# Split products for eight slots of the first input projection, with GpSimd making the lower weight parts

## The chip, the cores and the metric

The kernel runs on one core of one Trainium2 chip. The metric is the device time of one execution in microseconds. The kernel before takes 1461.06 us, the median of three runs (1459.4 to 1461.32).

## The reference, cut to what matters

Two transformer blocks over 256 tokens of width 1024, all in float32. The change touches the head of the first block:

```
mod = silu(c) @ w_ada + b_ada                  # 6 x 1024 values: shift1, scale1, gate1, shift2, scale2, gate2
h = rms_norm(x, g) * (1 + scale1) + shift1
proj = h @ w_in                                # 1024 -> 2320
q_g, k_g, v_g, a_lr, r_g, q_s, k_s, v_s = split(proj)
o_gla = gated linear attention(q_g, k_g, v_g, log_a(a_lr)); o_gla = rms_norm(o_gla) * silu(r_g)
o_swa = rms_norm(sliding window attention(q_s, k_s, v_s, sinks))
x = x + gate1 * (concatenate(o_gla, o_swa) @ w_out)
x = x + gate2 * peer(modulate(x, shift2, scale2))   # picks 128 experts per token, gathers their rows
```

Everything behind it (the PEER mixer with its gathered experts, a sparse-attention layer, two MLPs and a second attention layer) is untouched.

## The kernel before, in words

Each engine has its program written out by hand, and semaphores order the engines among each other. Weights come in slots of 512 KB (128 partitions x 1024 float32), which SyncE loads into a ring of four buffers. A slot n may be loaded when TensorE has used slot n-4 (`slots_used`).

The first input projection `w_in` has 18 slots, numbered 0 to 17. Each gives one 128 x 256 block of the projection in one half of the PSUM tile `pu` (`entry(e)`, two entries that take turns). ScalarE takes the block out (`evac`), and TensorE may begin slot i only when the blocks up to i-2 are out. `project` and `project_tokens` (lines 672 and 682) multiply in plain float32: eight matmuls of 128x256 (the profile records two for each). `up_slot` (line 709) is the other way, used further on for `w_out`, the MLPs and the second attention layer: the weights and the activations are each split in a high part of the type fp32r and a remainder (`ring_hi`, `ring_lo`, `Xh`, `Xl`), and `three` (line 703) makes three fp32r matmuls for each of the eight. `split_high` (line 450) is two ScalarE copies of 128x512 into `ring_hi`, which has two buffers, so the high part of slot n waits until slot n-2 is used. `split_low` (line 458) is two 128x512 subtractions, in place in the ring; in the kernel before VectorE makes them all.

Beside the slots of `w_in` run the sixteen units of the sliding window attention. From slot 6 (`EARLY`) on, each slot is followed on TensorE and on ScalarE by its share of the attention's steps (`steps_after`: 20 steps over 11 slots, two at most behind a slot). A unit goes from TensorE (scores, L877) to VectorE (bias L2139, maximum L2033), ScalarE (exponential, L1508), VectorE (reciprocal L2038, scaling L2044), TensorE (transposes L887), ScalarE (copy), TensorE (products L899), ScalarE (copy). On ScalarE, the exponentials of the gated linear attention (five activations) stand between the `evac` of slot 5 and that of slot 6.

The modulation is made on VectorE: `modulation` (line 2059) multiplies a row of `w_ada` (512 KB) with `silu(c)` and sums it up. Rows 0 to 15 have buffers of their own, and rows 16 to 39 go through `aring`, four buffers; row n may be loaded when row n-4 is used (`ada_used`). GpSimd issues them all (L542). VectorE takes rows 22 to 33 in the first twelve steps of the attention (`swa_filler`), rows 34 to 37 after the last step, masks the scores of the linear attention (L2157), and takes rows 38 and 39. Behind these in VectorE's order come the lower parts of the first `w_out` slot (L463), the reciprocal of the attention's norm (L2163), the scaling (L2165), the states of the linear attention (L2171, L2174), and then TensorE's products with the states (L1006) and the slots of `w_out`.

After `w_out` come the choice of the experts and 256 gathers of 1 MB each, which GpSimd issues (L581) into ten buffers.

Of the kernel before, what the change touches and what calls it, by code (L numbers as in the profile page):

```python
# [14 lines left out]
P = 128  # L15
# [54 lines left out]
SPLIT, _n = {}, 0  # L70
# [5 lines left out]
XSPLIT = {"w_out": 0, "a_o": 1, "b_in": 3, "b_o": 5}  # L76
# [13 lines left out]
EARLY, BESIDE = 6, 11  # L90

# [28 lines left out]
SEMS = """c_loaded x_loaded cols_loaded relb_loaded small_loaded xn_ready h_scaled h_chunks h2_sq h2_scaled h2_ready tile_done tile_out h2_copied consts_made casts_made c_silu ada_used chain_dve chain_act chain_pool slots_used evacs narrow_psum  # L120
# [10 lines left out]
def build(nc, xT_d, c_d, cols_d, ada_d, weights_d, small_d, alpha_d, keys_d, late_q_d, experts_d, relb_d, onehot_d, sinks_d, fin_row_d, w1_d, out_d):  # L131
    ctx = ExitStack()
    with ctx:
# [211 lines left out]

        def pair_landed(m):

            k = m % PAIR_SLOTS
            before = 0 if k < PAIR_SLOTS - ARING else 16 * ((MOD_EARLY - 2 * C) // ARING)
            return pair_full[k], before + 16 * (m // PAIR_SLOTS + 1)  # L350
# [93 lines left out]
        def tick(g, per_round, base):  # L444

            return base if g is None else g * per_round + base

        halves = (slice(0, 512), slice(512, D))
# [9 lines left out]
        def split_low(eng, api, name, k, g=None):  # L458

            n = SLOT[name] + k  # L460
            for j, half in enumerate(halves):
                eng.wait_ge(s["split_hi"], tick(g, 2 * BODY, 2 * (SPLIT[name] + k) + j + 1))
                api.tensor_tensor(ring_lo[:, n % RING, half], ring[:, n % RING, half],  # L463
                                  ring_hi[:, n % 2, half], ALU.subtract).then_inc(s["split_lo"], 1)
# [7 lines left out]
        def _(sp):  # L472
            for dst, src, sem in ((cols[:, :], cols_d, "cols_loaded"), (relb[0:NB, :], relb_d, "relb_loaded"),
                                  (oneh[0:NB, :], onehot_d, "relb_loaded"), (walr, small_d[:, :, 0:16], "small_loaded"),
                                  (walpha[0:16, :], alpha_d, "small_loaded"), (keysT, keys_d, "small_loaded"),
                                  (sinks[:, :], sinks_d.partition_broadcast(P), "small_loaded")):
                sp.dma_start(dst, src).then_inc(s[sem], 16)
# [31 lines left out]
        def _(pool):  # L509
# [28 lines left out]
            with pool.Fori(2 * C // ARING, MOD_EARLY // ARING) as g:  # L538
                for k in range(ARING):

                    pool.wait_ge(s["ada_used"], g * ARING + (k + 1 - ARING))
                    pool.dma_start(aring[:, k, :], ada_d[bass.ds(g * ARING + k, 1), :, :].rearrange("a p n -> (a p) n"))\  # L542
                        .then_inc(ada_full[k], 16)
# [121 lines left out]
        def _(pe):  # L665
# [33 lines left out]
            def split_ready(name, k, half, g):  # L699

                pe.wait_ge(s["split_lo"], tick(g, 2 * BODY, 2 * (SPLIT[name] + k) + half + 1))
# [151 lines left out]
            pe.wait_ge(s["relb_loaded"], 16 * 2)  # L853
# [118 lines left out]
            project(SLOT["w_in"] + 17, USE["w_in"] + 17, HTf)  # L972
# [526 lines left out]
        def _(act):  # L1499
# [86 lines left out]
            act.dma_start(cs, c_d.partition_broadcast(P)).then_inc(s["c_loaded"], 16)  # L1586
            act.dma_start(XT[:, :, :], xT_d).then_inc(s["x_loaded"], 16)
            act.wait_ge(s["casts_made"], 1)
            act.wait_ge(s["c_loaded"], 16)
            f(cs, cs, ACT.Silu).then_inc(s["c_silu"], 1)  # L1590
            act.wait_ge(s["x_loaded"], 16)
# [66 lines left out]
            evac(SLOT["w_in"] + 17, rs[:, 3, :], entry(USE["w_in"] + 17))  # L1658
            act.wait_ge(s["sums"], NORM["swa"])
# [329 lines left out]
        def _(dve):  # L1989
# [80 lines left out]
            dve.wait_ge(s["cols_loaded"], 16)  # L2070
            first = cols[:, COL["b_ada"]:COL["b_ada"] + 2 * C]
            step(v.tensor_scalar(strided(first[:, 0:1], [[2, C]]), strided(first[:, 0:1], [[2, C]]), 1.0, None, ALU.add))
            dve.wait_ge(s["relb_loaded"], 16 * 2)
# [44 lines left out]
            v.tensor_scalar(kp, kp, 80.0 * GATE_TEMP, None, ALU.min).then_inc(s["ex_ready"], 1)  # L2118

# [40 lines left out]
            modulation(2 * C + 22, 2)  # L2160
            split_low(dve, v, "w_out", 0)
# [680 lines left out]
```

## Time and profile before

| What | Value |
|---|---|
| Median of three runs | 1461.06 us (1459.4 to 1461.32) |
| The profiled execution's own time | 1459.02 us |
| Its span | 1457.4 us |
| TensorE busy | 1295.8 us (89%) |
| VectorE busy | 936.4 us (64%) |
| ScalarE busy | 658.5 us (45%) |
| GpSimd busy | 396.4 us (27%) |
| Granted TensorE clock, mean | 0.983 |

The profile is of one execution. Busy times are sums over the whole span, and engines work beside each other; 1.6 us of the execution's time lie outside the span. The chain of waits follows the work that ended last back from the last instruction, step by step.

### The profile page before, as it was taken

The page shows a single profiled execution, that of the slowest core. Times are in us where ns is not written, and L with a number is a line of the kernel's source. Part 1 is how long each engine was busy: PE and PEld are TensorE (multiplying, and loading weights), DVE is VectorE, ACT ScalarE, POOL GpSimd, SP SyncE. Part 2 cuts the span into 40 slices and gives each one's busy share as a digit, 9 for nine tenths or more (in the row PEclk, how much of TensorE's full clock was granted, in tenths as well). Part 3 has the DMA queues.
Part 4 walks back from the last instruction along what each step waited for, and adds up shares of the span by engine and source line. Part 5 has one row for each costly group of instructions (what it writes and reads, how often), then busy time and mean ns, then how long its engine had stood idle before and what let it go on. Part 6 is the DMA issues. An engine that isn't in the chain of part 4 may idle for free.

```text
span 1457.4 us, 21059 instructions
## 1 busy us (share of the span) xinstructions
PE 1295.8 (89%) x6856; PEld 930.2 (64%) x6856; DVE 936.4 (64%) x2259; ACT 658.5 (45%) x1809; POOL 396.4 (27%) x440
## 2 busy tenths in 40 slices
PE   6999888988888888777787888999999999999998
PEld 3888744434433343222332467899998887899897
DVE  6678787766767666766664566655556744655555
ACT  3444344443443434333433336555545448545554
POOL 4112345544444444444443142200001004100000
PEclk9999999999999999999999998999999999999999
DMA  8877799999999999999999621765556530455554
GB/s 330 339 265 282 272 420 420 421 423 420 421 422 421 420 421 421 422 421 422 421 421 422 246 74 43 255 203 181 184 187 240 193 116 2 159 161 186 186 187 145
DMA packets 81340, 422.50 MB, mean 290 GB/s; under 512 B 10144, under 2 KB 11472, under 8 KB 48368
## 3 DMA queue, kind: packets, MB, share of 16 engines
q0 software_dynamic: 47808, 307.91, 51.6%
q1 hardware_dynamic: 32128, 110.48, 22.7%
q10 hardware_dynamic: 1328, 3.15, 0.6%
q8 instruction: 41, 0.67, 0.2%
q14 instruction: 35, 0.29, 0.1%
HBM read 418.88 MB, written 2.62 MB: 289 GB/s over the span
## 4 chain that ended last, share of the span: by engine, by line
PE 54%; DMA 26%; DVE 11%; ACT 4%; issue 2%; POOL 1%; DVEq 0%; ACTq 0%; SPq 0%; POOLq 0%
DMA big<-in_experts,R 25%; PE pacc L1174 9%; PE pu L705 6%; PE pu L707 6%; PE pu L706 6%; PE pu L678 3%; DVE big L2477 3%; PE pacc L705 2%; PE pacc L706 2%; PE pacc L707 2%; PE pacc L763 2%; PE pacc L762 2%; PE pacc L764 2%; PE pu L688 1%; PE pu L1093 1%
## 5 line engine op out<-in xcount | busy, mean ns | idle before, releaser
L1174 PE MATMUL pacc<-big,early_l 128*128 128x512 f32 x1024 | 481.1, 612 | 106.8 <-ACT early_l L1508 106.8
L1174 PEld LDWEIGHTS pacc<-big,early_l 128*128 128x128 f32 x1024 | 187.3, 193 | 382.7 <-issue 380.2
L2477 DVE CUSTOM_DVE_ANT_0 big<-big,early_h 128x1024 f32<-128x1024 f32 x256 | 310.7, 1225 | 185.9 <-DMA big<-in_experts,R 184.7
L581 POOL DMA_INDIRECT big<-in_experts,R x256 | 289.5, 1131 | 363.6 <-PE pacc L1174 329.4
L463 DVE TENSOR_TENSOR ring_lo<-ring,ring_hi 128x512 fp32r<-128x512 f32 x336 | 220.0, 696 | 193.8 <-ACT ring_hi L456 193.6
L456 ACT ACTIVATE ring_hi<-ring 128x512 fp32r<-128x512 f32 x336 | 192.4, 620 | 135.2 <-PE pu L707 53.1
L1508 ACT ACTIVATE R<-R 128x1 f32<-128x1 f32 x256 | 51.4, 201 | 296.5 <-DVE R L2477 296.3
L705 PE MATMUL pu<-X2h,ring_hi 128*128 128x256 f32 x512 | 146.3, 286 | 3.2 <-DVE big L2592 3.2
L707 PE MATMUL pu<-X2h,ring_lo 128*128 128x256 f32 x512 | 145.5, 284 | 0.0
L706 PE MATMUL pu<-X2l,ring_hi 128*128 128x256 f32 x512 | 145.4, 284 | 0.0
L705 PEld LDWEIGHTS pu<-X2h,ring_hi 128*128 128x128 f32 x512 | 98.8, 193 | 4.3 <-DVE big L2592 3.6
L706 PEld LDWEIGHTS pu<-X2l,ring_hi 128*128 128x128 f32 x512 | 98.9, 193 | 0.3
L1508 ACT ACTIVATE early_l<-early_l,R 128x128 f32<-128x128 f32 x256 | 98.9, 386 | 0.1
L707 PEld LDWEIGHTS pu<-X2h,ring_lo 128*128 128x128 f32 x512 | 98.8, 193 | 0.0
L1508 ACT ACTIVATE early_l<-ident,tk 128x128 f32<-128x128 f32 x256 | 98.7, 387 | 0.0
L705 PE MATMUL pu<-Xh,ring_hi 128*128 128x256 f32 x288 | 85.7, 298 | 7.6 <-DVE Xl L2002 3.2
L707 PE MATMUL pu<-Xh,ring_lo 128*128 128x256 f32 x288 | 82.0, 285 | 0.0
L706 PE MATMUL pu<-Xl,ring_hi 128*128 128x256 f32 x288 | 82.0, 285 | 0.0
L705 PE MATMUL pacc<-act_h,ring_hi 128*128 128x256 f32 x256 | 72.2, 282 | 0.4 <-DVE ring_lo L463 0.4
L706 PE MATMUL pacc<-act_l,ring_hi 128*128 128x256 f32 x256 | 72.0, 281 | 0.0
L707 PE MATMUL pacc<-act_h,ring_lo 128*128 128x256 f32 x256 | 72.0, 281 | 0.0
L1508 ACT ACTIVATE big<-big 128x256 f32<-128x256 f32 (+3 forms) x74 | 34.1, 466 | 78.5 <-DVE big L2592 78.0
(433 smaller groups left out, 2101.1 us busy)
## 6 DMA issues: line engine op xcount, KB each, us to landing
ring<-in_weights SPq DMA_DIRECT2D x208, 512.0 KB, 3.5
big<-in_ada POOLq DMA_DIRECT2D x40, 512.0 KB, 6.4
big<-in_w POOLq DMA_DIRECT2D x12, 512.0 KB, 7.4
big<-in_experts,R POOLq DMA_INDIRECT x256, 19.3
big<-in_late_q POOLq DMA_DIRECT2D x6, 512.0 KB, 8.9
bias_row<-big ACTq DMA_DIRECT2D x1, 1536.0 KB, 19.9
XT<-in_xT ACTq DMA_DIRECT2D x1, 1024.0 KB, 8.2
scr<-in_ada POOLq DMA_DIRECT2D x2, 512.0 KB, 12.2
```

The source lines that it names most:

```text
L456: nc.scalar.activation(ring_hi[:, n % 2, half], ring[:, n % RING, half], ACT.Copy).then_inc(s["split_hi"], 1)
L463: api.tensor_tensor(ring_lo[:, n % RING, half], ring[:, n % RING, half], ring_hi[:, n % 2, half], ALU.subtract).then_inc(s["split_lo"], 1)
L581: pool.indirect_dma_start(out=pair_rows[:, m % PAIR_SLOTS, :], out_offset=None, in_=experts_d, in_offset=bass.IndirectOffsetOnAxis(ap=expe ...
L678: last = mm(entry(e), slot(n)[:, c * P:(c + 1) * P], rhs[:, c, :], start=(c == 0), stop=(c == C - 1))
L705: mm(out, ring_hi[:, n % 2, w], xh, start=start, stop=False, skip_group_check=True)
L706: mm(out, ring_hi[:, n % 2, w], xl, start=False, stop=False, skip_group_check=True)
L707: return mm(out, ring_lo[:, n % RING, w], xh, start=False, stop=stop, skip_group_check=True)
L762: mm(out, xh[:, rows], ring_hi[:, n % 2, w], start=False, stop=False, skip_group_check=True)
L763: mm(out, xl[:, rows], ring_hi[:, n % 2, w], start=False, stop=False, skip_group_check=True)
L1174: last = mm(paccf[:, tt * D + half * 512:tt * D + (half + 1) * 512], diagonal[:, m % 16, :], pair_rows[:, m % PAIR_SLOTS, D + half * 512:D ...
L1508: return nc.scalar.activation(out, in_, func, **k)
L2477: v.tensor_tensor_reduce(out=pair_rows[:, m % PAIR_SLOTS, 0:D], in0=pair_rows[:, m % PAIR_SLOTS, 0:D], in1=h2_rows[:, u % TT, :], scale=1. ...
```

## The change

Slots 6 to 9 and 14 to 17 of `w_in` go through `up_slot` in place of `project`. ScalarE makes their high parts two slots ahead (before the `evac` of slots 4 to 7 and 12 to 15), and the high parts `Xh` of the activations after the `evac` of slots 2 and 3. VectorE makes the lower parts `Xl` before the attention's first step. GpSimd makes the lower parts of the eight slots of weights. GpSimd now issues modulation rows 16 to 25 only, and ScalarE issues rows 26 to 37, each behind a step of the attention, and rows 38 and 39 behind the `evac` of slot 17. `split_no` numbers the split slots for the semaphores, and four semaphores of the first loads are used again for ScalarE's rows. VectorE waits for all sixteen lower parts before it makes the first ones of `w_out`.

```
-SPLIT, _n = {}, 0
+W_SPLIT = (6, 7, 8, 9, 14, 15, 16, 17)
+SPLIT, _n = {}, len(W_SPLIT)
+ACT_ROWS = 26
...
+        def act_row_landed(n):
+            k = n % ARING
+            before = 32 if k == 3 else 16
+            earlier = (n - ACT_ROWS) // ARING
+            return s[("c_then_row0", "x_then_row1", "cols_then_row2", "relb_then_row3")[k]], before + 16 * (earlier + 1)
...
+        def split_no(name, k):
+            return W_SPLIT.index(k) if name == "w_in" else SPLIT[name] + k
...   # GpSimd
-            with pool.Fori(2 * C // ARING, MOD_EARLY // ARING) as g:
-                for k in range(ARING):
-                    pool.wait_ge(s["ada_used"], g * ARING + (k + 1 - ARING))
-                    pool.dma_start(aring[:, k, :], ...).then_inc(ada_full[k], 16)
+            for n_row in range(2 * C, ACT_ROWS):
+                pool.wait_ge(s["ada_used"], n_row + 1 - ARING)
+                pool.dma_start(mod_row(n_row), ada_d[n_row, :, :]).then_inc(ada_full[n_row % ARING], 16)
+            for k in W_SPLIT:
+                split_low(pool, nc.gpsimd, "w_in", k)
...   # TensorE
+                elif i in W_SPLIT:
+                    up_slot("w_in", i, USE["w_in"] + i, None, 0, "w_in" if i == W_SPLIT[0] else None)
...
-            project(SLOT["w_in"] + 17, USE["w_in"] + 17, HTf)
+            up_slot("w_in", 17, USE["w_in"] + 17, None, 0)
...   # ScalarE
+            def row_in(n_row):
+                act.wait_ge(s["ada_used"], n_row + 1 - ARING)
+                sem, landed = act_row_landed(n_row)
+                act.dma_start(mod_row(n_row), ada_d[n_row, :, :]).then_inc(sem, 16)
+            def rows_in(i):
+                if ACT_ROWS <= ACT_ROWS - 1 + i < MOD_EARLY - 2:
+                    row_in(ACT_ROWS - 1 + i)
-            swa_step = attend("swa", swa_out, later=True)
+            swa_step = attend("swa", swa_out, rows_in, later=True)
...
+                if i + 2 in W_SPLIT:
+                    split_high(act, "w_in", i + 2)
...
+                if i in (2, 3):
+                    act.wait_ge(s["h_chunks"], C)
+                    x_high(HTf[:, 4 * (i - 2):4 * (i - 2) + 4, :], i - 2)
...
             evac(SLOT["w_in"] + 17, rs[:, 3, :], entry(USE["w_in"] + 17))
+            row_in(MOD_EARLY - 2)
+            row_in(MOD_EARLY - 1)
...   # VectorE
+                    elif n >= ACT_ROWS:
+                        dve.wait_ge(*act_row_landed(n))
...
             v.tensor_scalar(kp, kp, 80.0 * GATE_TEMP, None, ALU.min).then_inc(s["ex_ready"], 1)
+            both_low("w_in", HTf)
...
             modulation(2 * C + 22, 2)
+            dve.wait_ge(s["split_lo"], 2 * len(W_SPLIT))
             split_low(dve, v, "w_out", 0)
```

## Rows read from the trace of the kernel before

**Rows 1.** The page: GB/s moved in 40 slices of the span.

```profile
GB/s 330 339 265 282 272 420 420 421 423 420 421 422 421 420 421 421 422 421 422 421 421 422 246 74 43 255 203 181 184 187 240 193 116 2 159 161 186 186 187 145
```

**Rows 2.** The chain of waits, 36 to 135 us: start us, us, what.

```profile
43.14 14.01 PE pu L678 x64
...
68.68 3.65 PE pu L678 x16
...
119.05 1.74 PE pacc L969 x8
...
121.33 1.76 DVE R L2163
...
126.46 1.83 PE pacc L1006 x24
```

**Rows 3.** The chain of waits, 135 to 260 us: two split slots of w_out.

```profile
137.80 0.12 PE pu L705
...
143.43 0.12 PE pu L707
```

**Rows 4.** The timeline of ScalarE: start us, us, engine, line, operation, idle before.

```profile
44.05 0.40 ACTq L1612 DMA_DIRECT2D bias_row<-big  x1
...
62.46 3.57 ACT L1508 ACTIVATE big<-big 128x512 f32<-128x512 f32 x5
65.94 0.36 ACT L1508 ACTIVATE big<-pu 128x256 f32<-128x256 f32 x1
...
66.20 0.39 ACT L1508 ACTIVATE big<-big,stats 128x129 f32<-128x129 f32 x1
...
119.09 0.38 ACT L1508 ACTIVATE big<-pu 128x256 f32<-128x256 f32 x1 [0.99 <-PE pu L678]
...
121.75 1.14 ACT L456 ACTIVATE ring_hi<-ring 128x512 fp32r<-128x512 f32 x2
```

**Rows 5.** The timeline of VectorE in and behind the projection.

```profile
64.73 0.15 DVE L2138 COPY big<-sinks 128x1 f32<-128x1 f32 x1 [6.26 <-PE pn L877]
...
70.83 0.15 DVE L2138 COPY big<-sinks 128x1 f32<-128x1 f32 x1
...
126.32 1.22 DVE L2002 TENSOR_TENSOR Xl<-big,Xh 128x1024 fp32r<-128x1024 f32 x1
```

**Rows 6.** Line 638: GpSimd's subtractions' nearest kin; duration ns min/median/max.

```profile
L638 POOL TENSOR_TENSOR big<-big x16: 455/593/737, 875.2 to 888.0; 128x128 f32<-128x128 f32 x8, 128x256 f32<-128x256 f32 x8
```

**Rows 7.** The timeline of GpSimd and VectorE, 1213 to 1216 us.

```profile
1213.37 1.27 DVE L463 TENSOR_TENSOR ring_lo<-ring,ring_hi 128x512 fp32r<-128x512 f32 x2
1213.56 1.44 POOL L655 TENSOR_SCALAR big<-big,stats 128x256 f32<-128x256 f32 x1 [0.35 <-DVE stats L2038]
...
1215.16 0.56 POOL L655 TENSOR_SCALAR big<-big,stats 128x256 f32<-128x256 f32 x1 [0.17 <-DVE stats L2038]
```

**Rows 8.** The timeline, 110 to 120 us: modulation rows 38 and 39.

```profile
110.76 0.53 POOL L542 DMA_DIRECT2D big<-in_ada  x1 [12.20 <-DVE mod L2067]
...
116.08 1.23 DVE L2067 CUSTOM_DVE_ANT_0 big<-big 128x1024 f32<-128x1024 f32 x1 [1.06 <-DMA big<-in_ada]
...
118.36 1.23 DVE L2067 CUSTOM_DVE_ANT_0 big<-big 128x1024 f32<-128x1024 f32 x1 [1.05 <-DMA big<-in_ada]
...
119.51 1.29 DVE L463 TENSOR_TENSOR ring_lo<-ring,ring_hi 128x512 fp32r<-128x512 f32 x2
```

**Rows 9.** DMA issues, 100 to 120 us: KB each, median us to landing.

```profile
ring<-in_weights SPq DMA_DIRECT2D x4, 512.0 KB, 4.0
big<-in_ada POOLq DMA_DIRECT2D x2, 512.0 KB, 5.9
```

**Rows 10.** The timeline of TensorE at 902 us: a start after idle time.

```profile
902.34 0.35 PE L705 MATMUL pu<-Xh,ring_hi 128*128 128x256 f32 x1 [2.46 <-DVE Xl L2002]
```

**Rows 11.** Windows of 1 us: busy PE, PEld, DVE, ACT, POOL; then granted clock, DMA share, GB/s.

```profile
903.00:904.00 1.00, 1.00 (x7) 1.00 (x6) 1.00 (x3) 0.00 (x0) 0.00 (x0) 0.50 0.02 8
...
906.00:907.00 1.00, 1.00 (x10) 1.00 (x9) 0.02 (x1) 0.00 (x0) 0.00 (x0) 0.95 0.00 0
```

More of the change, by code:

```diff
@@ L74 @@
         _n += 4 if _name == "w_out" else _k
-XSPLIT = {"w_out": 0, "a_o": 1, "b_in": 3, "b_o": 5}
+XSPLIT = {"w_in": 0, "w_out": 2, "a_o": 3, "b_in": 5, "b_o": 7}
 RAW = {n: C * i for i, n in enumerate(["mlp0", "kv", "mlp1"])}
@@ L118 @@
 NSA_OUT = OUTNO[SPAN["nsa"][0]]
[L120 removed]
+SEMS = """c_then_row0 x_then_row1 cols_then_row2 relb_then_row3 small_loaded xn_ready h_scaled h_chunks h2_sq h2_scaled h2_ready tile_done tile_out h2_copied consts_made casts_made c_silu ada_used chain_dve chain_act chain_pool slots_used evacs narrow_psum
 narrow_copied z_psum squares sums roots normed la_parts ex_ready ex_done silu_done gla_ops kl_psum kl_copied gla_scores
@@ L344, in pair_column @@
             return u % TT * P + u // TT * TOPK + m % TOPK
+        def act_row_landed(n):
[3 more added lines that the diff above has]
+            return s[("c_then_row0", "x_then_row1", "cols_then_row2", "relb_then_row3")[k]], before + 16 * (earlier + 1)
         def pair_landed(m):
             k = m % PAIR_SLOTS
-            before = 0 if k < PAIR_SLOTS - ARING else 16 * ((MOD_EARLY - 2 * C) // ARING)
+            before = 0 if k < PAIR_SLOTS - ARING else 16 * len(range(2 * C + (k + ARING - PAIR_SLOTS), ACT_ROWS, ARING))
             return pair_full[k], before + 16 * (m // PAIR_SLOTS + 1)
@@ L461, in split_low @@
             for j, half in enumerate(halves):
-                eng.wait_ge(s["split_hi"], tick(g, 2 * BODY, 2 * (SPLIT[name] + k) + j + 1))
+                eng.wait_ge(s["split_hi"], tick(g, 2 * BODY, 2 * split_no(name, k) + j + 1))
                 api.tensor_tensor(ring_lo[:, n % RING, half], ring[:, n % RING, half],
@@ L472, in _ @@
         def _(sp):
-            for dst, src, sem in ((cols[:, :], cols_d, "cols_loaded"), (relb[0:NB, :], relb_d, "relb_loaded"),
-                                  (oneh[0:NB, :], onehot_d, "relb_loaded"), (walr, small_d[:, :, 0:16], "small_loaded"),
+            for dst, src, sem in ((cols[:, :], cols_d, "cols_then_row2"), (relb[0:NB, :], relb_d, "relb_then_row3"),
+                                  (oneh[0:NB, :], onehot_d, "relb_then_row3"), (walr, small_d[:, :, 0:16], "small_loaded"),
                                   (walpha[0:16, :], alpha_d, "small_loaded"), (keysT, keys_d, "small_loaded"),
@@ L699, in split_ready @@
             def split_ready(name, k, half, g):
-                pe.wait_ge(s["split_lo"], tick(g, 2 * BODY, 2 * (SPLIT[name] + k) + half + 1))
+                pe.wait_ge(s["split_lo"], tick(g, 2 * BODY, 2 * split_no(name, k) + half + 1))
             def three(out, n, w, xh, xl, start, stop):
@@ L852, in _ @@
             last.then_inc(s["spreads"], 1)
-            pe.wait_ge(s["relb_loaded"], 16 * 2)
+            pe.wait_ge(s["relb_then_row3"], 16 * 2)
             pe.wait_ge(s["relb_spread"], 1)
@@ L1584, in attend @@
                     one(st)
-            act.dma_start(cs, c_d.partition_broadcast(P)).then_inc(s["c_loaded"], 16)
-            act.dma_start(XT[:, :, :], xT_d).then_inc(s["x_loaded"], 16)
+            act.dma_start(cs, c_d.partition_broadcast(P)).then_inc(s["c_then_row0"], 16)
+            act.dma_start(XT[:, :, :], xT_d).then_inc(s["x_then_row1"], 16)
             act.wait_ge(s["casts_made"], 1)
-            act.wait_ge(s["c_loaded"], 16)
+            act.wait_ge(s["c_then_row0"], 16)
             f(cs, cs, ACT.Silu).then_inc(s["c_silu"], 1)
-            act.wait_ge(s["x_loaded"], 16)
+            act.wait_ge(s["x_then_row1"], 16)
             squares(XT[:, :, :], sq[:, :, :])
@@ L2068, in modulation @@
                                            op0=ALU.mult, op1=ALU.add, accum_out=mod[:, n:n + 1]).then_inc(s["ada_used"], 1)
-            dve.wait_ge(s["cols_loaded"], 16)
+            dve.wait_ge(s["cols_then_row2"], 16)
             first = cols[:, COL["b_ada"]:COL["b_ada"] + 2 * C]
             step(v.tensor_scalar(strided(first[:, 0:1], [[2, C]]), strided(first[:, 0:1], [[2, C]]), 1.0, None, ALU.add))
-            dve.wait_ge(s["relb_loaded"], 16 * 2)
+            dve.wait_ge(s["relb_then_row3"], 16 * 2)
             v.tensor_copy(relb_all[0:NB, :, :], strided(relb[0:NB, 0:1], [[1, NH], [0, P]])).then_inc(s["relb_spread"], 1)
```

2 lines of the change are left out of this document (removed).

## The prediction

> **What bounds the kernel now.** I read the page's throughput slices first. From the sixth slice (about 182 us) to the 22nd (about 800 us) the DMA engines move 420 to 423 GB/s without a break [rows 1]: these are the gathers of the experts, and their number is fixed. They start when the head of the kernel has chosen the first experts. So what moves the head moves the end by as much, and nothing is caught up behind it. The chain of waits says what the head consists of. From 43 to 119 us it is TensorE, slot after slot of the projection [rows 2]; then it leaves TensorE: sums of squares at 119.05, a root on ScalarE, VectorE's reciprocal at 121.33, VectorE's scaling and states, and TensorE again at 126.46. Two facts decide: how early slot 17 ends, and how early VectorE can start that reciprocal. The timeline of VectorE shows that the second has little room: it takes modulation rows 38 and 39 at 116.08 and 118.36, each after idle time for its DMA, then 1.29 us of lower parts until 120.80 [rows 8]. It is free 0.53 us before it is needed.
>
> **The change part by part.**
>
> *Products.* Four plain slots take 14.01 us, 3.50 each [rows 2]. Two split slots of the same shape take 143.55 - 137.80 = 5.75 us, 2.88 each [rows 3]. Eight slots times 0.62 us is 5.0 us of TensorE time, the most that the change can give.
>
> *Activation parts.* VectorE's part is 2 x 1.22 us by the one row of this shape; it falls into the 6.26 us in which VectorE is idle before the first attention unit [rows 5]. ScalarE's part is of the same size, between evacuations of slots 2 to 4. Cost nothing; without the cover it would be up to 2.4 us.
>
> *High parts.* Each slot adds 1.14 us to ScalarE [rows 4], and they stand ahead of evacuations. Those of slots 7 and 8 come before the evacuations of slots 5 and 6, with the five exponentials (62.46 to 66.03) between them. So the evacuation of slot 6 moves from 65.94 by 2 x 1.14 and a little to about 68.5, and the first unit's exponential from 66.20 to about 68.9 [rows 4]. Slot 8 needs that evacuation and began at 68.68 [rows 2]. It can't begin earlier: the 1.24 us that slots 6 and 7 gain are gone. The late exponential also holds up VectorE, whose unit 3 stood at 70.83 [rows 5]; it moves to about 73.2, and TensorE needs it for the scores behind slot 8, whose end stood at 72.33. I put TensorE 1 to 2.5 us behind its old time when it enters the plain slots 10 to 13. Slots 14 to 16 win 1.86 back in part, since VectorE's units are then as tight as TensorE. Slot 17 stands behind the last attention step and gives its full 0.62. I take slot 17's evacuation to end 0.9 us earlier than its 119.47 [rows 4], at 118.5. The bounds are 5.0 us earlier (nothing given back) and 1.5 us later.
>
> *Lower parts on GpSimd.* The trace has no such 128x512 subtraction on GpSimd. Its nearest row runs from 0.46 us at 128 columns to 0.74 at 256 [rows 6]: an estimate of 0.46 + 3 x 0.28 = 1.3 us each, 2.6 us a slot. The lower bound is VectorE's 0.64 us for the same operation [rows 7], the upper twice my value. By 1.3 us a half is ready some 2 us after ScalarE's start and the other 1.3 later. That is on time for slots with attention steps between them, more than 3 us apart, so alone it costs nothing; at twice the price each of the eight slots would wait up to 2 us.
>
> GpSimd and VectorE get in each other's way: a scaling that takes 0.56 us alone takes 1.44 when VectorE has two subtractions of lower parts running [rows 7]. The Trainium skill says why ("SBUF — State Buffer", section "SBUF: two separate sides"): a VectorE operation with two SBUF inputs and a GpSimd operation that reads SBUF exclude each other for a whole instruction. By that rule, every modulation row and every gate product of the linear attention can stand against a GpSimd half. From the row alone, each split slot then costs VectorE up to 1.3 us and GpSimd up to 1.2 in addition; over the four slots 6 to 9 this is at most 5 us, part of it on the path. I take it as the upper half of the 1 to 2.5 us above; it is the third case below in full.
>
> *Modulation rows 26 to 37.* ScalarE's issue is 0.40 us each [rows 4], twelve of them 4.8 us, spread over steps in which ScalarE is half idle. By its order, ScalarE issues row 25+i behind the exponential of unit i, and this waits for VectorE, which has used row 21+i by then: no new wait. They start a little later than now and have three units to land. At most one stall of 1 us in VectorE, nothing on the sum.
>
> *Modulation rows 38 and 39.* Now GpSimd issues row 38 at 110.76, and the two take 5.9 us in the median to land [rows 8, 9]. After the change ScalarE issues them behind the evacuation of slot 17: 118.5 and 118.9. Ring loads of the same size took 4.0 us in this stretch and modulation rows 5.9 [rows 9]; with a ring load and both rows at once I take 4.9 for row 39. It lands at 123.8. VectorE stands at row 38 and then at row 39, with the lower parts and the reciprocal queued behind: 123.8 + 1.2 (row 39) + 1.3 (lower parts) = 126.3, against 121.33. All that follows on VectorE and the states' products on TensorE wait for that: **+5.0 us**. ScalarE's own delay (two issues of 0.40 ahead of the root) is inside it. Nothing hides it, since TensorE has only its filler matmuls there.
>
> *Clock.* TensorE's work ahead of the states' products doesn't wait for the rows and is earlier than before, while those products move from 126.46 [rows 2] to about 131.5; so TensorE gets 5 us or more of idle time. After 2.46 us of idle time the granted clock was 0.50 (1.2 GHz) at 903 and on its way back in the microsecond from 906 [rows 10, 11]. There some three microseconds ran at half speed, which is 1.5 us of work not done. I add **+1.5 us**.
>
> Sum: -0 (the products' gain is inside the 118.5) + 5.0 + 1.5 = +6.5 us on the profiled execution's 1459.02 us, 1465.5. The median of the runs stands 2.04 above the profiled execution, so the forecast is 1467.5 us; I give 1467.
>
> **The rivals.**
>
> *Late rows, but mild.* Slot 17's evacuation ends at 115.5, the rows land in 4 us and the clock doesn't fall. Row 39 is issued at 115.9 and lands at 119.9, and the reciprocal starts at 122.4: +1.1. With half of that luck it is +3. For it: slots 14 to 17 could keep their 2.5 us. Against it: the late exponentials. Time 1462 to 1464.5.
>
> *The shared access decides.* GpSimd's halves and VectorE's rows hold each other up in each of the eight slots, and TensorE waits for second halves. Slot 17 ends 3 to 5 us late (four slots x 1.2 us, less what the plain slots absorb), and the rows come later by the same: +10 to +12, 1471 to 1473. For it: the 1.44 us [rows 7]. Against it: the spaces between the units.
>
> *The products win (other side).* The place is VectorE at the reciprocal. If row 39 were to land before about 115.5, VectorE would be free before the root, and the earlier end of slot 17 would pass: -3 to -5, 1456 to 1458. This decides from an evacuation of slot 17 at about 111, and even the whole 5.0 us of gain brings only 114.5. What could break my reading is time downstream that absorbs the delay, of which rows 1 show none.
>
> *The change doesn't do what it says.* If GpSimd's halves are always the last to come, split slots run no faster than plain ones. This is then the third case with less price, and I leave its chance there.
>
> **How the numbers follow.** Late rows with the clock's fall 0.58 (own range 1464.5 to 1470), mild late rows 0.25, shared access 0.12, products win 0.05. The range 1462.3 to 1472 leaves out the last case, the best of the mild one and the far end of the third. A measurement of this kernel can tell 0.2%, 2.9 us, from no change. Faster by that is the products' case, 0.05. Within it lies half of the mild case, 0.13. Slower is the rest, 0.82.
>
> **What would show it.** L678's groups of 16 are replaced by L705 to L707 of `Xh` in slots 6 to 9 and 14 to 17, 2.9 us each. VectorE's unit 3 stands near 73. In VectorE's timeline, two modulation rows wait for a DMA between 115 and 124, and the reciprocal L2163 starts near 126. TensorE has idle time before L1006, and the granted clock is 0.50 behind it. The first gather comes about 6.5 us later than now, and all behind it by the same. Wrong would be: L2163 before 122, a clock of 1.00 after L1006, or a delay at L1006 that isn't found at the first gather.

## The result, and the profile after

The changed kernel takes 1480.07 us (median of 6 runs, 1476.44 to 1484.22) against 1461.42 us for the kernel before, measured beside it: a ratio of 1.0127 with a 95% interval of 1.0114 to 1.0141. That is 18.7 us slower, where 6 were forecast. The profiled execution took 1480.23 us with a span of 1478.5 us, 21.1 us more than before; its mean granted clock is 0.976 (before 0.983).

The page after, the line that answers to [rows 1] and those on the modulation rows. The gathers run as fast as before and end later. The rows that ScalarE issues have a line of their own now:

```profile
GB/s 330 320 256 214 172 399 416 421 422 421 422 421 421 421 421 421 421 421 421 422 421 422 279 113 47 196 234 183 184 184 208 237 116 12 157 152 188 184 185 144
...
big<-in_ada POOLq DMA_DIRECT2D x26, 512.0 KB, 8.3
...
big<-in_ada ACTq DMA_DIRECT2D x14, 512.0 KB, 4.7
```

The timeline of ScalarE after, beside [rows 4]. The evacuation of slot 6 and the first unit's exponential are 2.15 us later (68.09, 68.35), and the evacuation of slot 17 ends at 126.12. Behind it stand the issues of modulation rows 38 and 39:

```profile
68.09 0.37 ACT L1523 ACTIVATE big<-pu 128x256 f32<-128x256 f32 x1
68.35 0.39 ACT L1523 ACTIVATE big<-big,stats 128x129 f32<-128x129 f32 x1
...
125.74 0.38 ACT L1523 ACTIVATE big<-pu 128x256 f32<-128x256 f32 x1 [0.40 <-PE pu L720]
125.75 0.82 ACTq L1639 DMA_DIRECT2D big<-in_ada  x2
```

The timeline of VectorE after, beside [rows 8]. Two modulation rows (L2102) take 2.29 and 2.28 us where the same row takes 1.22; then come 5.70 us of waiting for row 38, 0.83 for row 39, the lower parts, and the reciprocal:

```profile
117.86 2.29 DVE L2102 CUSTOM_DVE_ANT_0 big<-big 128x1024 f32<-128x1024 f32 x1
120.08 2.28 DVE L2102 CUSTOM_DVE_ANT_0 big<-big 128x1024 f32<-128x1024 f32 x1
...
129.87 1.23 DVE L2102 CUSTOM_DVE_ANT_0 big<-big 128x1024 f32<-128x1024 f32 x1 [5.70 <-DMA big<-in_ada]
131.94 1.23 DVE L2102 CUSTOM_DVE_ANT_0 big<-big 128x1024 f32<-128x1024 f32 x1 [0.83 <-DMA big<-in_ada]
133.09 1.29 DVE L477 TENSOR_TENSOR ring_lo<-ring,ring_hi 128x512 fp32r<-128x512 f32 x2
134.29 1.75 DVE L2200 RECIPROCAL R<-R 128x256 f32<-128x256 f32 x1
```

The chain of waits after, beside [rows 2]: from the evacuation it goes through the DMA of the modulation rows to VectorE's reciprocal, and to the states' products, which took 1.83 us before and take 3.31 now:

```profile
125.74 0.34 ACT big L1523
126.12 5.79 DMA big<-in_ada
...
134.38 1.67 DVE R L2200
...
139.42 3.31 PE pacc L1021 x24
```

TensorE in windows of 2 us, after (busy PE, PEld, DVE, ACT, POOL; granted clock, DMA share, GB/s). In the kernel before the clock is 1.00 from 56 to 136 us. Here TensorE is idle for most of 72 to 76 and of 106 to 108, and its clock falls to 0.50 (1.2 GHz) behind both. VectorE is busy for 1.93 us or more of every two from 72 to 82 us and from 102 to 108 us:

```profile
72.00:74.00 2.00, 0.55 (x5) 0.34 (x3) 1.93 (x8) 0.68 (x3) 1.81 (x1) 1.00 0.72 281
74.00:76.00 2.00, 0.55 (x5) 0.47 (x6) 1.93 (x8) 0.09 (x1) 0.00 (x0) 1.00 0.92 356
76.00:78.00 2.00, 2.00 (x14) 2.00 (x15) 1.93 (x8) 1.05 (x5) 0.00 (x0) 0.71 0.66 209
78.00:80.00 2.00, 2.00 (x11) 2.00 (x11) 1.93 (x8) 0.27 (x2) 0.00 (x0) 0.50 0.83 295
80.00:82.00 2.00, 2.00 (x17) 1.40 (x16) 1.94 (x6) 0.46 (x2) 0.00 (x0) 0.93 0.63 188
...
106.00:108.00 2.00, 0.35 (x2) 0.39 (x4) 1.97 (x5) 0.00 (x0) 0.56 (x1) 0.89 0.87 272
108.00:110.00 2.00, 2.00 (x10) 1.02 (x10) 1.79 (x6) 0.00 (x0) 0.00 (x0) 0.50 0.58 234
110.00:112.00 2.00, 2.00 (x17) 1.67 (x18) 0.00 (x0) 0.94 (x5) 0.00 (x0) 0.75 0.00 0
```

What TensorE waited for, in its own timeline after, are scores (L890). It can't write them before VectorE has read the scores that stand in the same PSUM bank (L2175):

```profile
75.45 0.34 PE L890 MATMUL pm<-big 64*128 64x128 f32 x1 [2.90 <-DVE big L2175]
...
107.65 0.76 PE L890 MATMUL pm<-big 64*128 64x256 f32 x1 [2.31 <-DVE big L2175]
```

How far TensorE had come when it began slot 10, the first of the plain slots in the middle. The lines are of before, of after, and of e13, the changed kernel without the lower parts (see the experiments):

```profile
77.67 3.84 PE L688 MATMUL pu<-ring,big 128*128 128x128 f32 x32
```

```profile
81.76 3.84 PE L701 MATMUL pu<-ring,big 128*128 128x128 f32 x32
```

```profile
78.78 3.84 PE L699 MATMUL pu<-ring,big 128*128 128x128 f32 x32
```

The kernel in five marks, for every kernel of this study (us from the start, from each profiled execution). "w_out" is the first 128x128 product behind the first split slots of `w_out` (before: L1020, behind [rows 3]):

| Kernel | slot 17 out | reciprocal | w_out | first gather | span | ratio of times |
|---|---|---|---|---|---|---|
| before | 119.5 | 121.3 | 143.4 | 164.3 | 1457.4 | 1 |
| after | 126.1 | 134.3 | 160.4 | 183.9 | 1478.5 | 1.0127 |
| e1 rows only | 119.5 | 127.7 | 153.5 | 174.4 | 1471.2 | 1.0083 |
| e2 VectorE makes lower parts | 126.0 | 134.1 | 159.9 | 182.9 | 1476.3 | 1.0119 |
| e3 rows 38, 39 earlier | 125.1 | 130.5 | 156.2 | 177.1 | 1470.6 | 1.0104 |
| e4 50 fillers | 127.8 | 136.0 | 161.1 | 184.5 | 1477.9 | 1.0121 |
| e5 split only | 125.3 | 128.1 | 151.7 | 174.2 | 1468.4 | 1.0065 |
| e6 split 14 to 17 | 121.9 | 125.2 | 150.3 | 172.9 | 1466.4 | 1.0052 |
| e7 split 6 to 9 | 123.2 | 125.1 | 147.2 | 169.7 | 1462.9 | 1.0040 |
| e8 high parts behind | 125.1 | 129.1 | 152.7 | 175.2 | 1468.8 | 1.0088 |
| e9 products alone | 116.4 | 118.3 | 140.3 | 163.2 | 1456.9 | 0.9988 |
| e10 no lower parts | 118.2 | 120.1 | 142.1 | 165.3 | 1459.2 | 1.0002 |
| e11 rows only, 70 fillers | 119.5 | 127.8 | 149.9 | 173.0 | 1466.0 | 1.0041 |
| e12 = e2 and e3 | 126.2 | 129.5 | 153.1 | 175.6 | 1468.4 | 1.0080 |
| e13 rows, no lower parts | 118.5 | 126.9 | 152.4 | 174.9 | 1469.5 | 1.0069 |
| e14 lower products last | 125.5 | 133.5 | 158.7 | 181.8 | 1475.0 | 1.0115 |
| e15 = e5, lower products last | 124.7 | 128.1 | 152.9 | 175.4 | 1468.9 | 1.0082 |
| e16 after, 70 fillers | 127.1 | 135.3 | 157.5 | 178.4 | 1471.9 | 1.0098 |

The marks are of one execution each. Up to slot 17, after, e4 and e16 run the same program, and slot 17 ends at 126.1, 127.8 and 127.1 us; so among the kernels with GpSimd's lower parts, a difference of under 2 us at this mark shows nothing. For e1 and e11, the same program without split slots, it is 119.5 both times.

### The profile page after: what moved, and what is told of

It is laid out like the page before. It is cut to its first block, busy times and chain, and to the rows that moved or that the text cites. A ratio compares the mean times of both kernels' runs of the same rounds, so it can differ in the third digit from the quotient of the medians.

```text
span 1478.5 us, 21151 instructions
## 1 busy us (share of the span) xinstructions
PE 1298.3 (88%) x6920; PEld 937.4 (63%) x6920; DVE 949.1 (64%) x2261; ACT 668.4 (45%) x1827; POOL 421.9 (29%) x442
## 4 chain that ended last, share of the span: by engine, by line
PE 52%; DMA 27%; DVE 12%; ACT 5%; issue 3%; POOL 1%; DVEq 0%; ACTq 0%; SPq 0%; POOLq 0%
DMA big<-in_experts,R 25%; PE pacc L1189 8%; PE pu L718 6%; PE pu L720 6%; PE pu L719 6%; DVE big L2514 3%; PE pacc L776 2%; PE pacc L775 2%; PE pacc L777 2%; PE pacc L718 2%; PE pacc L719 2%; PE pacc L720 2%; DMA ring<-in_weights 1%; DVE ring_lo L477 1%; PE pu L1108 1%
## 5 line engine op out<-in xcount | busy, mean ns | idle before, releaser
L594 POOL DMA_INDIRECT big<-in_experts,R x256 | 295.5, 1154 | 360.1 <-PE pacc L1189 324.1
L470 ACT ACTIVATE ring_hi<-ring 128x512 fp32r<-128x512 f32 x352 | 201.5, 620 | 141.0 <-PE pu L720 53.5
L718 PE MATMUL pu<-Xh,ring_hi 128*128 128x256 f32 x352 | 106.6, 303 | 9.2 <-DVE Xl L2035 4.9
L720 PE MATMUL pu<-Xh,ring_lo 128*128 128x256 f32 x352 | 101.9, 289 | 0.0
L719 PE MATMUL pu<-Xl,ring_hi 128*128 128x256 f32 x352 | 101.9, 289 | 0.0
L718 PEld LDWEIGHTS pu<-Xh,ring_hi 128*128 128x128 f32 x352 | 69.8, 198 | 15.8 <-issue 12.5
```

Source lines behind the costliest of these rows:

```text
L470: nc.scalar.activation(ring_hi[:, n % 2, half], ring[:, n % RING, half], ACT.Copy).then_inc(s["split_hi"], 1)
L594: pool.indirect_dma_start(out=pair_rows[:, m % PAIR_SLOTS, :], out_offset=None, in_=experts_d, in_offset=bass.IndirectOffsetOnAxis(ap=expe ...
L718: mm(out, ring_hi[:, n % 2, w], xh, start=start, stop=False, skip_group_check=True)
L719: mm(out, ring_hi[:, n % 2, w], xl, start=False, stop=False, skip_group_check=True)
L720: return mm(out, ring_lo[:, n % RING, w], xh, start=False, stop=stop, skip_group_check=True)
```

## The experiments

Each is an edit of the changed kernel. The ratios are to the kernel before on the same chip.

**e1, the moved rows alone.** All slots plain again, ScalarE still issues rows 26 to 39.

```
-W_SPLIT = (6, 7, 8, 9, 14, 15, 16, 17)
+W_SPLIT = ()
```

> Only the moved modulation rows are kept: ScalarE issues rows 26 to 39, and all 18 slots are plain products again, with no parts made. Theory L (rows 38 and 39 behind slot 17 cost by themselves): slot 17 ends at its old 119.05, the reciprocal starts 8.3 us behind its evacuation as in the changed kernel, at about 127.8, the clock falls once, and the time is 9 to 12 us above before. Theory P (GpSimd and VectorE holding each other up is the main cost): the rows are a small part, under 5 us above before.

1472.59 against 1460.09 us, 1.0083 (1.0067 to 1.0100). Slot 17 ends where it did before, and the issue stands at 119.13 in place of 110.76. VectorE's timeline:

```profile
123.26 1.22 DVE L2099 CUSTOM_DVE_ANT_0 big<-big 128x1024 f32<-128x1024 f32 x1 [8.22 <-DMA big<-in_ada]
125.29 1.22 DVE L2099 CUSTOM_DVE_ANT_0 big<-big 128x1024 f32<-128x1024 f32 x1 [0.79 <-DMA big<-in_ada]
...
127.65 1.74 DVE L2195 RECIPROCAL R<-R 128x256 f32<-128x256 f32 x1
```

Fourteen issues were moved, and the delay in the head begins with the last two: 6.3 us to the reciprocal, and 3.8 more between it and w_out, with the clock at 0.50 from 130 to 140 us. The first gather comes the same 10.1 us later. The time is 12.5 us longer, and the span of the profiled execution 13.8; of this, 3.7 us lie behind the first gather, where the work is that of before, and where they come from stays open.

**e2, the lower parts on VectorE.** GpSimd's loop goes; VectorE makes the parts of slots 6 and 7 ahead of the attention and the others in six of its steps.

```
-            for k in W_SPLIT:
-                split_low(pool, nc.gpsimd, "w_in", k)
+            split_low(dve, v, "w_in", 6)
             both_low("w_in", HTf)
+            split_low(dve, v, "w_in", 7)
...
+                if i in LOWER_AT:
+                    split_low(dve, v, "w_in", LOWER_AT[i])
```

> The changed kernel with the eight slots' lower parts on VectorE instead of GpSimd, in its own order (16 subtractions of 0.64 us). Theory P: the VectorE operations of 2.3 us go back to 1.2, slot 17 ends 4 to 7 us earlier than in the changed kernel, and the time is 4 to 8 us below it. Theory L: VectorE carries 10 us more work, slot 17 is no earlier, and the time stays within 2 us of the changed kernel's 1480.

1477.78 against 1460.09, 1.0119 (1.0102 to 1.0136): within 0.1% of the change. Theory P was right that VectorE's long operations go back (from 62 to 122 us a modulation row takes 1218 ns in the mean), and wrong that time comes back with them. To take GpSimd away is worth nothing when VectorE has to do its work. What this leaves open (does GpSimd's work cost VectorE as much as VectorE's own?) is settled by e13.

**e3, rows 38 and 39 earlier.** ScalarE issues them ahead of its last attention step.

```
+            row_in(MOD_EARLY - 2)
+            row_in(MOD_EARLY - 1)
             swa_step(SPAN["swa"][1] + 4)
...
-            row_in(MOD_EARLY - 2)
-            row_in(MOD_EARLY - 1)
```

> The changed kernel with rows 38 and 39 issued by ScalarE ahead of the last attention step (about 121.8) instead of behind slot 17's evacuation (125.8). Theory L: both rows are there by about 127, the reciprocal starts near 129.5 instead of 134.4, TensorE's idle time shrinks from 6.7 to about 2 us, and the time is 5 to 9 us below the changed kernel's. If another wait of VectorE takes their place, the gain is under 2 us.

1475.08, 1.0104 (1.0087 to 1.0121), and the reciprocal 3.8 us earlier than after the change. By the ratios this is 3.4 us less than the change, by the medians 5.0, at the lower edge of the 5 to 9 expected or below it. The place of the two issues on ScalarE is a price of its own, but most of the loss stays.

**e4, 50 filler matmuls ahead of the states' products in place of 6.**

```
-            full_array(6, entry(USE["w_out"]))
+            full_array(50, entry(USE["w_out"]))
```

> The changed kernel with 50 filler matmuls in place of 6 ahead of the states' products, 0.107 us each, so that TensorE works through its 6.7 us of idle time. If the clock's fall costs what the two traces show (states' products 3.31 us against 1.83, first w_out slot 2 us longer), the time is 3 to 4 us below the changed kernel's; if it costs 1.5 us as predicted, 1 to 2 us.

1478.28, 1.0121 (1.0104 to 1.0138). Inconclusive: the fillers ended early. The states' products still stood behind 1.88 us of idle time, and the clock fell (TensorE's timeline and the windows of this kernel):

```profile
133.82 5.40 PE L978 MATMUL pu<-zeros 128*128 128x256 bf16 x48
141.10 2.70 PE L1021 MATMUL pacc<-big 64*128 64x64 f32 x24 [1.88 <-DVE big L2211]
```

```profile
140.00:142.00 2.00, 0.90 (x12) 0.90 (x13) 1.97 (x5) 1.98 (x4) 0.00 (x0) 0.96 1.01 414
142.00:144.00 2.00, 2.00 (x16) 1.88 (x16) 1.55 (x4) 1.86 (x2) 0.00 (x0) 0.50 1.03 422
```

**e5, the split alone.** e2, and GpSimd issues all modulation rows again.

```
-ACT_ROWS = 26
+ACT_ROWS = 40
...
-            row_in(MOD_EARLY - 2)
-            row_in(MOD_EARLY - 1)
```

> Split products alone: all eight slots are split, lower parts on VectorE, and GpSimd issues all modulation rows as before. If the costs add up (rows alone were 12.5 us above before, the kernel with VectorE's lower parts 17.7), this is about 5 us above before, slot 17's evacuation ends 5 to 7 us later than before's 119.5, and VectorE is free at the reciprocal. Rival: the rows issued by ScalarE also slowed the steps, and without them slot 17 ends within 1 us of before and the time is within 2 us of it.

1470.66 against 1461.87, 1.0065 (1.0052 to 1.0078). The waits of this kernel, 56 to 130 us (waited in us, times, longest), name VectorE's units:

```profile
PE pm L888 <- DVE big L2173: 7.5, 5, 2.4
```

**e6 and e7, half of the split.** e5 with `W_SPLIT = (14, 15, 16, 17)` and with `W_SPLIT = (6, 7, 8, 9)`.

> As the run before, but only slots 14 to 17 are split. Theory S (the high parts ahead of the evacuations and exponentials set the pace of the attention units): half of the loss, slot 17 ends 1 to 3 us later than before, time 0 to 3 us above. If the loss is in slots 6 to 9 alone, slot 17 ends 0.5 to 2 us earlier and the time is 0 to 2 us below before.

> As the first of these, but only slots 6 to 9 are split. Theory S: the plain slots 10 to 13 begin 3 to 4 us later than before's 77.7, which passes to slot 17, and the time is 3 to 4 us above before. The rival: the plain slots take it up, and the time is within 1.5 us of before.

1469.25, 1.0052 (1.0032 to 1.0072), and 1467.05, 1.0040 (1.0025 to 1.0054). Neither half pays. At slot 17 they add up (2.4 and 3.8 us later than before, e5 5.8). The times add up to 0.0092, for e5's 0.0065, which is within the intervals. From the reciprocal to w_out, e6 takes 25.1 us and e5 23.5, both with a part at half clock, and e7 22.1, as before.

**e8, the high parts behind the evacuations.** In e5, ScalarE's `split_high` of slot i + 2 moves from ahead of the evacuation of slot i to behind it.

> As the first of these, with ScalarE making each high part behind the evacuation of the same turn instead of ahead of it. The order against the evacuation gates slot 8 by 1.1 us at most: theory S, by which it is the exponentials behind both that are late, expects under 1 us of difference to the first; if the evacuation is what counts, the time is 1.5 to 3 us below it.

1473.56, 1.0088 (1.0073 to 1.0103): not faster than e5. Whether it is slower isn't clear, since the intervals overlap. Slot 17 ends 0.2 us earlier. The order on ScalarE isn't the loss.

**e9 and e10, parts left out.** e9 is e5 without any high or lower parts of the eight slots' weights: the three products read `Xh` in the weights' place (their weights don't enter the result). e10 makes the high parts and leaves out the lower ones: all three products read `ring_hi`.

```
-                    last = three(entry(e), n, slice(c * P, (c + 1) * P), ...)
+                        hi = ring_hi[:, n % 2, w]          # e9: Xh[:, c, 0:P]
+                        mm(entry(e), hi, xs[0][:, c, :], ...)
+                        mm(entry(e), hi, xs[1][:, c, :], ...)
+                        last = mm(entry(e), hi, xs[0][:, c, :], ...)
```

> The 24 fp32r products of the eight slots alone: no high or lower parts of their weights are made by any engine, and these products read a block of Xh in the weights' place (the computation of w_in's weights is left out for the eight slots; each still waits for its slot). Modulation rows are issued by GpSimd as before. If the products are worth what the rows say (8 x 0.62 us) and nothing else binds, slot 17 ends 4 to 5 us earlier and the time is 3 to 5 us below before. If VectorE's units bind in slots 12 to 16, slot 17 ends 1.5 to 3 us earlier.

> As the run before, but ScalarE makes the high parts and all three products read them; no lower parts are made (the lower parts of these weights are left out). Theory A (ScalarE's high parts ahead of the exponentials are the loss): time within 2 us of the kernel with all parts and VectorE's lower parts (8.8 above before), 6 us or more above before. Theory B (the lower parts are the loss, on whichever of the two engines): within 2.5 us of before, or below it.

1459.24 against 1460.59, 0.9988 (0.9974 to 1.0003), and 1460.87, 1.0002 (0.9990 to 1.0013). Slot 17's evacuation in each:

```profile
116.01 0.38 ACT L1532 ACTIVATE big<-pu 128x256 f32<-128x256 f32 x1 [0.40 <-PE pu L738]
```

```profile
117.84 0.38 ACT L1532 ACTIVATE big<-pu 128x256 f32<-128x256 f32 x1 [0.40 <-PE pu L738]
```

At slot 17 the products gain 3.1 us of the 5.0, and the high parts take 1.8 of it back. The lower parts, made by VectorE, then cost 7.1 us at slot 17 (125.3 in e5, 118.2 in e10), and 9.2 us of time (1.0065 against 1.0002). That is theory B.

**e11, e1 with 70 fillers.**

> The kernel with only the moved modulation rows (12.5 us above before) and 70 filler matmuls in place of 6, which fill TensorE's whole idle time of 6.7 us. If the clock's fall costs the 3.8 us that the trace shows between the reciprocal and the tiles behind w_out's fourth slot, the time is 3 to 4 us below that kernel's, about 8.5 above before.

1467.74 against 1460.59, 1.0041 (1.0025 to 1.0056). The clock holds (windows of e1, then of e11):

```profile
130.00:135.00 5.00, 2.23 (x19) 2.23 (x20) 4.93 (x11) 3.84 (x5) 0.00 (x0) 0.50 1.02 404
135.00:140.00 5.00, 5.00 (x27) 4.88 (x26) 3.83 (x10) 2.87 (x3) 0.00 (x0) 0.50 0.20 82
```

```profile
130.00:135.00 5.00, 5.00 (x54) 4.44 (x53) 4.93 (x12) 3.68 (x5) 0.00 (x0) 1.00 1.03 411
135.00:140.00 5.00, 5.00 (x45) 5.00 (x45) 4.06 (x11) 3.44 (x5) 0.00 (x0) 1.00 0.42 145
```

The reciprocal stays late (127.80), and w_out comes 22.1 us behind it in place of 25.9: there the clock's fall cost 3.8 us. The times of e1 and e11 differ by 0.0042, 6 us (4.9 by the medians of the two series), but this isn't all shown to be the clock's. At the first gather e11 is 1.4 us ahead of e1, since behind w_out the clock falls in e11 and not in e1, and e11 waits there for a weight load too (see the part on why the prediction was wrong). The other 3.8 us by which its span is shorter lie behind the first gather.

**e12, VectorE's lower parts and the earlier rows together.**

> Lower parts on VectorE and rows 38 and 39 ahead of the last attention step. The same pair without the row's move differed by 2.3 us (1480.1 and 1477.8). If GpSimd's share in the loss is that small, this is 1 to 3 us below the 1475.1 of GpSimd's lower parts with the same rows. What is left above the kernel with GpSimd's rows (8.8 above before) is what ScalarE's issue of rows 26 to 39 costs without the late place: 1 to 4 us.

1471.87, 1.0080 (1.0061 to 1.0099). That is near the split alone (e5, 1.0065), and within the intervals: with the rows in time, nothing clear of noise is left beside the split's price.

**e13, the changed kernel without the lower parts.** As e10, with the rows left on ScalarE (the lower parts don't enter the result).

> The changed kernel without the lower parts: GpSimd makes none, and the three products of the eight split slots read the high parts (the lower parts of these weights are left out of the result). Modulation rows 26 to 39 stay with ScalarE. Theory B (the lower parts themselves are the price of the split): slot 17's evacuation comes back from 126.1 to about 118.2, where it stood with high parts only, the reciprocal starts near 126.4 and the kernel takes about 8 us less than the changed one, near 1472. Rival (the late rows cost more because the split slots are there): over 1475.

1471.57 against 1461.95, 1.0069 (1.0044 to 1.0093). Against the change this is 8.5 us less (0.0058 of the time). VectorE's groups from 62 to 122 us (busy us, mean ns; after, then e13) show the price:

```profile
L2102 DVE CUSTOM_DVE_ANT_0 big<-big 128x1024 f32<-128x1024 f32 x15 | 21.4, 1434 | 0.0
L2077 DVE TENSOR_SCALAR big<-big,stats 128x128 f32<-128x128 f32 (+1 forms) x16 | 8.1, 504 | 0.6
...
L2167 DVE TENSOR_TENSOR big<-big 128x512 f32<-128x512 f32 x4 | 3.8, 952 | 0.0
```

```profile
L2111 DVE CUSTOM_DVE_ANT_0 big<-big 128x1024 f32<-128x1024 f32 x16 | 19.3, 1220 | 0.0
...
L2086 DVE TENSOR_SCALAR big<-big,stats 128x128 f32<-128x128 f32 (+1 forms) x16 | 5.1, 320 | 0.6
L2176 DVE TENSOR_TENSOR big<-big 128x512 f32<-128x512 f32 x4 | 2.7, 684 | 0.0
```

The same instructions are longer when GpSimd subtracts beside them: 15 rows x 0.214 + 16 scalings x 0.184 + 4 gate products x 0.268 = 7.2 us. A fifth gate product (1.75 for 0.69) and the activations' two lower parts (2.29 and 2.30 for 1.22) add 1.1 each: 10.4 us in all, of which 4.6 beside slots 6 to 9 and the rest beside 14 to 17. VectorE's own sixteen subtractions are 10.3 us in e5. This is why e2 changed nothing: VectorE pays about the same either way.

**e14 and e15, the lower products last.** In the changed kernel and in e5, each split slot makes its sixteen products with the high parts first, and waits for the lower halves only then.

```
+                    for c in range(C):
+                        ... pe.wait_ge(s["split_hi"], ...) at c = 0 and 4
+                        for y in xs:
+                            mm(entry(e), ring_hi[...], y[:, c, :], ...)
+                    for c in range(C):
+                        ... split_ready(name, k, c // 4, g) at c = 0 and 4
+                        last = mm(entry(e), ring_lo[...], xs[0][:, c, :], ...)
```

> The changed kernel, but in the eight split slots TensorE makes the sixteen products with the high parts first and the eight with the lower parts last, so that it waits for GpSimd's halves up to 1.9 us later in each slot; every instruction is still made. Theory W (TensorE's wait for the halves is what costs): slot 17's evacuation comes 4 us or more earlier than 126.1 and the kernel takes 1475 to 1476. Theory X (GpSimd's subtractions hold up VectorE, and the late units hold up TensorE): less than 2 us are won, 1478 to 1480.

> All eight slots split, VectorE makes the lower parts, GpSimd issues the modulation rows as before, and the products with the lower parts come last in each slot. With the products in the old order this took 1470.7 (slot 17's evacuation 125.3). Theory W: 1465 to 1467. Theory X (the 16 subtractions stand in VectorE's chain of units): over 1469. If it came under 1461 the split would pay.

1478.31 against 1461.95, 1.0115 (1.0090 to 1.0140), and 1473.56, 1.0082 (1.0061 to 1.0103). Slot 17 ends 0.6 us earlier in both, and the time of neither can be told from that of the kernel with the old order. TensorE's wait for the halves isn't the loss; it goes on to wait for the units.

**e16, the changed kernel with 70 fillers.**

> The changed kernel with 70 filler matmuls in place of 6 ahead of the states' products. The 50 fillers of before ended 1.9 us too early and the clock fell all the same. If the clock's fall is paid once and is the same as with the rows alone (4.9 us by the two runs with plain slots), this kernel takes 4 to 5 us less than the changed one, 1475 to 1476, at a clock of 1.00 from 130 to 148 us. Rival (the fall costs less here, because other waits take its place): 1478 or more.

1475.41 against 1461.95, 1.0098 (1.0075 to 1.0122). From 132 to 148 us, the windows of after and then of e16:

```profile
132.00:148.00 16.00, 9.27 (x55) 8.84 (x54) 13.43 (x26) 6.71 (x7) 2.61 (x5) 0.59 0.69 275
```

```profile
132.00:148.00 16.00, 16.00 (x160) 14.89 (x159) 13.96 (x31) 7.50 (x10) 2.61 (x5) 1.00 0.81 321
```

From the reciprocal to w_out it takes 22.3 us (after 26.1, before 22.1), and the time is 4.2 us less than that of the change (0.0029). At the first gather of the profiled executions e16 is 5.5 us ahead: 3.9 by this stretch, 2.6 in the one behind it, less the 1.0 by which its slot 17 ended later.

## Why the prediction was wrong in size

The direction and the late rows were right; two terms of the sum were much too small. In the profiled executions the 21.1 us of span are: slot 17 6.6 us later; 6.3 more from there to the reciprocal (8.2 in place of 1.9); 4.1 more to w_out; 2.6 to the first gather; 1.5 behind it.

*Products, at most -5.0:* right as a bound. Alone they bring 3.1 us at slot 17 (e9) and 1.4 us of time, which can't be told from none.

*Activation parts, 0:* right for the parts alone. In e13, without GpSimd's halves, they take 2.36 us and the first unit starts at 64.02, for 64.73 before. Beside GpSimd's first halves they took 4.52 us and not 2.4 (their row begins at 59.27), TensorE waited 1.7 us for them at slot 6, and the first unit starts at 66.15. That belongs to the lower parts.

*High parts:* right. Slot 6's evacuation ends at 68.46 for 68.5 forecast, the exponential starts at 68.35 for 68.9, and without lower parts VectorE's unit 3 is at 72.89 (e13) for 73.2. In the changed kernel itself it is at 74.96. The price of the high parts is 1.8 us at slot 17 (e10 less e9).

*Lower parts, inside "1 to 2.5 us behind", with slot 17's evacuation "0.9 us earlier":* this is the step that failed. It ended 6.6 us later, at 126.1, 7.6 us from the forecast's 118.5 and beyond the upper bound of 1.5. By the runs the 6.6 are -3.1 (products) + 1.8 (high parts) + 7.9 (lower parts: 126.1 less 118.2). Without the lower parts the forecast holds: slot 17 ends at 118.2 in e10 and at 118.5 in e13. The same shows at slot 10, where 1 to 2.5 us of delay were forecast: it is 1.1 in e13 and 4.1 after. The duration was right: GpSimd needs 2.56 us for two halves where it is VectorE that waits, for 1.3 each forecast. Where GpSimd waits too, two take 4.46 (timeline of GpSimd after):

```profile
104.00 2.56 POOL L477 TENSOR_TENSOR ring_lo<-ring,ring_hi 128x512 fp32r<-128x512 f32 x2 [2.78 <-ACT ring_hi L470]
...
116.81 4.46 POOL L477 TENSOR_TENSOR ring_lo<-ring,ring_hi 128x512 fp32r<-128x512 f32 x2 [1.15 <-ACT ring_hi L470]
```

The 1.44 us of [rows 7] showed that VectorE and GpSimd shut each other out, and the third case rested on it. For slots 6 to 9 I had taken 5 us on VectorE as the most, and 4.6 were measured, the activation parts among them, so this size was right. What I missed is where that lands, and that slots 14 to 17 pay it once more. I let the gaps between units absorb it, but from 72 to 82 us VectorE has no gap: a unit there is five small operations and a modulation row, 2.1 us from sink copy to sink copy, and 1.93 of every 2 us are busy. Whatever is added to VectorE, as its own instruction or as time shut out, moves every later unit, and TensorE's scores wait for it. TensorE then waits 2.90 and 2.31 us, and its clock falls to half behind both waits, where the same kernel without lower parts (e13) keeps 1.00 from 72 to 82 and from 102 to 114. By the windows from 76 to 82 and from 108 to 112, this is 3.2 us of work not done, part of the 7.9. It also fits that slots 6 to 9 alone cost 3.8 us at slot 17 (e7), although the plain slots 10 to 13 lie between: e7 begins slot 10 3.8 us later than before, and nothing of it is caught up.

The rule of the Trainium skill on this ("SBUF — State Buffer", section "SBUF: two separate sides") speaks of a full block for a whole instruction: 1.22 + 1.28 us would make 2.5 for a modulation row, and the longest are 2.29 to 2.33. The trace agrees with the rule.

*Rows 26 to 37, no new stall:* right. VectorE's waits from 60 to 130 us name the modulation's DMA once, for row 38.

*Rows 38 and 39:* right. From slot 17's end to the reciprocal 7.8 us were forecast (118.5 to 126.3); it took 8.2, and 8.2 in e1 too. The +5.0 was so small only because slot 17 was taken to be early: with slot 17 unmoved, as in e1, it is 6.3.

*Clock, +1.5:* the mechanism was right, the size was not. From the reciprocal to w_out, kernels whose clock holds there (before, e7, e9, e10, e11, e16) take 22.0 to 22.3 us, and after, e1 and e13 take 26.1, 25.9 and 25.6: 3.5 to 4.1 us. I had taken three microseconds at half speed from [rows 11]; in e1 the clock was 0.50 from 130 to 140 us, and TensorE worked for 7.2 of them. A second fall, which the sum didn't have, is in the next point. The whole times give 4 us (e16) and 6 (e11), and the 6 hold the 3.8 us behind the first gather that the clock of the head isn't shown to make.

*All behind it passes to the end:* right in the main; 2.6 + 1.5 us more were lost there. The 2.6 can be read in the traces. From w_out to the first gather, before, e1, e3 and e16 take 20.9 us, and TensorE's clock stays at 1.00. In all the others it is at 0.50 for some 3 us in the products ahead of the choice of the experts, and that adds 1.6 us (e5 to e8, e12, e13 and e15: 22.5 or 22.6). Where TensorE waits for a load of the weight ring as well, 0.4 to 1.0 us come on top (e9 22.9, after 23.5, with an idle time of 0.83 us). The same stretch, before and then after:

```profile
155.00:159.00 4.00, 4.00 (x38) 4.00 (x37) 3.99 (x12) 2.43 (x9) 0.00 (x0) 1.00 0.41 133
```

```profile
172.00:176.00 4.00, 4.00 (x24) 4.00 (x23) 3.35 (x12) 2.87 (x9) 0.00 (x0) 0.57 0.03 7
```

Why the clock falls there in some kernels and not in others stays open. So does the 1.5 us behind the first gather: all kernels but e1 take 1292.8 to 1294.6 us there, before 1293.1 and after 1294.6.

Do the parts add up? Rows alone 0.0083 and split alone 0.0065 are 0.0148, and the change has 0.0127, which is within the intervals. If there is a difference, the clock's fall behind slot 17, which both e1 and e5 have in some measure, may be paid once; that wasn't tried. The moved rows cost the same with split slots and high parts beside them (e13 less e10: 0.0067) as without, within the intervals. Of the rivals, the one on shared access had the mechanism of the larger error, with slot 17 3 to 5 us late in place of 6.6. Its second part, that TensorE waits for second halves, isn't what costs: the trace after has no such wait from 56 to 130 us, and e14 took no less time. That the change doesn't do what it says is refuted: the split slots' matmuls are there and faster.

No kernel here beats the one before for certain. e9, which leaves work out, is the limit of what faster products could bring in this place: 0.12%, with an interval that holds zero.

## What to carry to other kernels

Before work goes to a "free" engine, look at the engine that it shares memory access with: if that one is busy for 1.9 of every 2 us in the stretch, the work costs as much as if it were put there directly. A DMA issue that is moved behind the event that opens the critical path puts its landing time on that path, less the slack that there was: here 8.2 us in place of 1.9, for two rows that took 4.9 us in the median to land. And where a stall adds a few microseconds of idle time on TensorE, count the clock's fall by the work that follows at half speed on the path until it is back (7.2 us of it in e1), not by the first place in the trace where one was seen.

## What the runs showed of the hardware beyond what was expected

- An fp32 scaling of VectorE by a column of numbers, with one tensor as input, is lengthened by GpSimd's subtractions too: 504 ns in the mean for 320 (L2077 after, L2086 in e13), and single ones 1.35 to 1.38 us.
- The clock fell behind 1.88 us of idle time in e4, where 48 fillers had run until then, and stayed at 0.50 from 142 to 148 us.
- Three fp32r products in place of a plain float32 one shorten a slot of eight from 3.50 to 2.88 us, but eight such slots bring only 3.1 us at slot 17 (e9). That the attention's units beside them then set the pace is likely, but no run shows it.
